# Two mixer blocks of a one-core network: two sparse-attention units' scores and maxima moved ahead of the state-space heads

## The chip, the cores and the metric

The kernel runs on one core of one Trainium2 chip. The metric is the device time of one execution in microseconds (us), as the median of three runs. Engines are called by their names: TensorE (PE in the profile), VectorE (DVE), ScalarE (ACT), GpSimd (POOL) and SyncE (SP, which issues the DMAs of weights).

## The reference, cut to what matters

The program is a two-layer block (state-space mixer, short convolution, sparse attention, gated feed-forward) followed by a second network. The change touches only the mixers of the two layers of the first block. There 256 tokens of 1024 features are projected by `w_in`, three mixers run on parts of the projection, and their outputs, side by side, go through `w_out`:

```python
for l in range(DEPTH):
    h = rmsnorm(x, attn_norm_w[l])
    proj = h @ w_in[l]
    ...
    y_ssd = ssd_mixer(z, xbc, dt_raw, ...)       # 8 heads of 64, 2 groups, state 128
    y_sc = sc_b * causal_dwconv(sc_c * sc_h, sc_conv_w[l])
    y_nsa = nsa_mixer(q, k_c, v_c, k_s, v_s, k_w, v_w, g_nsa, ...)   # 4 heads of 64
    x = x + jnp.concatenate([y_ssd, y_sc, y_nsa], axis=-1) @ w_out[l]
```

In the state-space mixer a head's output is `(decay * cb) @ xdt` with `decay = exp(segment sums)`; in the sparse attention each query block has a softmax over 15 compressed keys, one over the selected keys and one over the window (at 256 tokens both of these see the same causal keys), and the three outputs are summed by gates.

## The kernel before, in words

Weights are float32. Each weight panel of 128x2048 is loaded into one of four `raw` slots by SyncE (slot after slot, L469 waits until the slot of four transfers ago is free), copied by ScalarE into a high part (`high`, L1317), and VectorE subtracts to give the low part (`low`, L1991); there are two slots of high and low parts, so `high` of a panel waits until the panel two before it has been used by TensorE. A product is three matmuls (`mm3`, L509): high by high, high by low, low by high. TensorE is the engine on which nearly all time is spent.

Every engine has its own queue, written out by hand in the order in which it runs (`mixers(l)` exists once for TensorE, L812; ScalarE, L1640; VectorE, L2461). There is no planner: an instruction late in its queue cannot pass one before it. Semaphores tie the queues together.

On TensorE the projection by `w_in` is cut into steps (`in_steps(a, b)`, L828): a step is one `mm3` of 256 columns, 16 steps make a panel, panels are counted j = 0 to 11, so panel j holds the steps 16j to 16j+15. From panel 9 on all panels write bank 0: step 160 waits until ScalarE has evacuated panel 9, step 176 until it has evacuated panel 10 (L835). Between groups of steps stand the small matmuls of the mixers:

- `scores(u)`, L883: scores of sparse unit u (there are 4: two pairs of heads by two blocks of 128 queries; units 0 and 2 see 128 keys and are called narrow here, 1 and 3 see 256 and are called wide). It waits for the maxima of unit u-1, because all units use banks 2 and 3; the compressed scores stand in `compressed(u)`, L437.
- VectorE's `maxes(u)`, L2621, ScalarE's `exps(u)`, L1728, VectorE's `probs(u)`, L2636, TensorE's `flips(u)`, L952 (transposes), ScalarE's `copies(u)`, L1740, TensorE's `product(u)`, L970, ScalarE's `out(u)`, L1750: the chain of one unit.
- `spread(t)`, L929, ScalarE's `ssd_gap(t)` and `ssd_exp(t)`, L1712 and L1723, VectorE's `mats(t)`, L2663, TensorE's `head_pair(t)`, L941, VectorE's `out(t)`, L2669: the chain of one of the four pairs of state-space heads. Banks 2 to 5 alternate for `spread`.
- In layer 0 alone, `spread_condition(i)`, L874, and ScalarE's `condition(i)`, L1671, prepare the second network's condition vector; the group matmuls of g = 1 (L923) wait for the last of them, as they take bank 7.
- At the end `norm(4, ...)`, L1025, sums the squares of the state-space output, and `out_part(n, MIXED)`, L987, starts the output projection: its eight inputs k come in the order `MIXED` = 6, 4, 5, 0, 1, 2, 3, 7, where 6 and 7 are sparse attention, 4 and 5 the short convolution and 0 to 3 the state-space output. Step k waits for the low part of input k (`mixed_low`, L2675).

ScalarE evacuates a finished panel (`evacuate(j)`, L1647) and makes the high part of the panel two later (`ahead(j)`, L1664); the order of ScalarE's queue from the first pair of heads on is written out from L1766. VectorE's is from L2681. The lines in ScalarE's queue that the steps below lean on, and which stand after the part that the change edits, are:

```python
evacuate(10)
copies(1)
ahead(10)
exps(3)
out(1)
copies(2)
run(root_warm[:, :], eps[:, :], ACT.Sqrt)
evacuate(11)
out(2)
nsa_high(0)
root_y()
copies(3)
```

Of the kernel before, what the change touches and what calls it, by code (L numbers as in the profile page):

```python
# [12 lines left out]
P = 128  # L13
# [230 lines left out]
def two_blocks(nc, xT, ctxT, params_d, consts_d, weights, out_d):  # L244
    ctx = ExitStack()
    with ctx:
# [75 lines left out]
        cond_diag = sb("cond_diag", [P, 2, 512], at=A + 4096)  # L322
# [114 lines left out]
        def compressed(u):  # L437

            return bank[1][:, 0:2 * N_CMP] if u else bank[2][:, T:T + 2 * N_CMP]
# [62 lines left out]
        def _(pe):  # L502
# [309 lines left out]
            def mixers(l):  # L812
# [70 lines left out]
                def scores(u):  # L883
                    i, _, qs, W = nsa_unit(u)
                    if u == 0:
                        pe.wait_ge(S("kv_ready"), l + 1)
                    else:
                        pe.wait_ge(S("nsa_max"), n0 + u)
                    if u == 1:
                        pe.wait_ge(S("ssd_gap"), d + 3)  # L890
                    for r in range(2):
                        for h2, rows in enumerate(halves):
                            mm(bank[2 + h2][:, r * W:(r + 1) * W], krq[rows, 2 + i, qs], krq[rows, r ^ h2, 0:W], True, True)
                    mm(compressed(u), krq[:, 2 + i, qs], kc[:, :, :].rearrange("p h n -> p (h n)"), True,
                       True).then_inc(S("nsa_scored"), 1)
# [15 lines left out]
                in_steps(132, 144)  # L911
                spread_condition(3)
# [3 lines left out]
                for tb in range(2):  # L916
                    for t in range(4):
                        last = nc.tensor.transpose(bank[4 + tb][:, t * P:(t + 1) * P], xc[:, t, tb * P:(tb + 1) * P], ident)
                    last.then_inc(S("x_turned"), 1)
                pe.wait_ge(S("xbc_ready"), x + 8)  # L920
                pe.wait_ge(S("kv_ready"), l + 1)
# [7 lines left out]
                def spread(t):  # L929
                    if t == 0:  # L930
                        pe.wait_ge(S("nsa_max"), n0 + 1)
# [76 lines left out]
                scores(1)  # L1008
                in_steps(160, 162)
                head_pair(3)  # L1010
                flips(0)
                in_steps(162, 166)
                scores(2)
                product(0)
                in_steps(166, 176)
                flips(1)
                scores(3)
                in_steps(176, 182)
                product(1)
                flips(2)  # L1020
                in_steps(182, 188)
                product(2)
                in_steps(188, 192)
                pe.wait_ge(S("nsa_max"), n0 + 4)
                norm(4, T, 512, o=1)  # L1025
                flips(3)
                product(3)
                ws[0] = panel(L + "_out", 0)
                pe.wait_ge(S("in_evac"), e + IN_PANELS)
                out_part(0, MIXED)  # L1030
# [277 lines left out]
        def _(act):  # L1308
# [331 lines left out]
            def mixers(l):  # L1640
# [125 lines left out]
                exps(0)  # L1766
                ssd_gap(0)
                ssd_exp(0)
                ssd_gap(1)
                ssd_exp(1)  # L1770
                ahead(8)
                ssd_gap(2)
                ssd_exp(2)
                evacuate(9)
                ssd_gap(3)
                ssd_exp(3)
                ahead(9)
                copies(0)
                exps(1)
# [203 lines left out]
        def _(dve):  # L1983
# [15 lines left out]

            def entry_low(name, n, i):  # L2000
# [27 lines left out]
            def mod_part(name, n, s):  # L2028
# [6 lines left out]
                link(V.tensor_tensor_reduce(products[:, :], raw[slot][:, 0:DM], cond[:, s, :], 1.0,  # L2035
# [425 lines left out]
            def mixers(l):  # L2461
# [110 lines left out]
                def in_low(j):  # L2572
                    low(f"l{l}_in", IN_ORDER[j])
# [108 lines left out]
                in_low(9)  # L2682
                for tb in range(2):
# [7 lines left out]
                if l:  # L2691
                    mod_part("l1_in", IN_ORDER[7], 0)
                else:
                    probs(0)
                mats(0)
                if l:
                    mod_part("l1_in", IN_ORDER[7], 1)
                mats(1)
                in_low(10)
                out(0)  # L2700
                mats(2)
                out(1)
                if l:
                    probs(0)
                mats(3)
                out(2)
                maxes(1)
                out(3)
                maxes(2)
                in_low(11)  # L2710
                probs(1)
                probs(2)
                maxes(3)
                short_conv(0)
                short_conv(1)
                probs(3)
# [4 lines left out]
                rms(4, T)  # L2721
                y2 = take("ssd_high", 4)
# [3 lines left out]
                mixed_low(0)  # L2726
                mixed_low(1)
# [369 lines left out]
```

## Time and profile before

| what | value |
|---|---|
| median of three runs | 2322.64 us (2322.52 to 2324.76) |
| time of the profiled execution | 2321.22 us |
| its span in the trace | 2319.4 us |
| TensorE, VectorE, ScalarE busy | 2263.3, 1699.2, 948.2 us |
| mixers of layer 0 from its last projection panels to the output projection | about 76 to 129 us |
| the same in layer 1 | about 408 to 460 us |

Times in the rows are us from the start of the span. A row of the timeline gives the start, the length, the engine, the source line, the operation with what it writes and reads, how many instructions were merged, and in brackets how long the engine had been idle before it and whom it waited for. Matmuls overlap, and the end of one is modelled: the distance from one start to the next is the time that TensorE's queue really takes, and an idle time in brackets is some 0.15 us shorter than the delay of the start. Line L507 is the helper of all matmuls and L1312 that of all ScalarE operations, so rows are told apart by their tiles: `sb_decays` are the state-space heads, `sb_nP` and `sb_nPT` the sparse units, `sb_hx_hi` with `sb_w_hi` projection steps.

### The profile page before, as it was taken

The page shows a single profiled execution, that of the slowest core. Times are in us where ns is not written, and L with a number is a line of the kernel's source. Part 1 is how long each engine was busy: PE and PEld are TensorE (multiplying, and loading weights), DVE is VectorE, ACT ScalarE, POOL GpSimd, SP SyncE. Part 2 cuts the span into 40 slices and gives each one's busy share as a digit, 9 for nine tenths or more (in the row PEclk, how much of TensorE's full clock was granted, in tenths as well). Part 3 has the DMA queues.
Part 4 walks back from the last instruction along what each step waited for, and adds up shares of the span by engine and source line. Part 5 has one row for each costly group of instructions (what it writes and reads, how often), then busy time and mean ns, then how long its engine had stood idle before and what let it go on. Part 6 is the DMA issues. An engine that isn't in the chain of part 4 may idle for free.

```text
span 2319.4 us, 35091 instructions
## 1 busy us (share of the span) xinstructions
PE 2263.3 (98%) x14334; PEld 2007.8 (87%) x14334; DVE 1699.2 (73%) x2781; ACT 948.2 (41%) x1408; POOL 112.7 (5%) x77
## 2 busy tenths in 40 slices
PE   7999999899999999999999999999999999999998
PEld 7799999799998888888778888888888888979997
DVE  6889978889989848845455883884884663796775
ACT  4766635766652222235553221222321222475343
POOL 0010010010110000010001000001000001001001
PEclk9999999999999999999999999999999999999999
DMA  6445475355545545532111553453454452313443
GB/s 248 164 146 182 156 257 190 116 200 183 175 170 192 189 154 182 181 127 87 51 73 55 182 186 129 166 182 127 147 196 157 137 176 105 144 40 124 181 157 121
DMA packets 66560, 355.83 MB, mean 153 GB/s; under 512 B 7136, under 2 KB 10208, under 8 KB 42336
## 3 DMA queue, kind: packets, MB, share of 16 engines
q1 hardware_dynamic: 66400, 353.60, 43.7%
q8 instruction: 113, 1.85, 0.3%
q14 instruction: 47, 0.39, 0.0%
HBM read 352.52 MB, written 1.05 MB: 152 GB/s over the span
## 4 chain that ended last, share of the span: by engine, by line
PE 87%; DVE 9%; ACT 2%; issue 1%; DMA 0%; DVEq 0%; ACTq 0%
PE bank L507 87%; DVE sb_w_lo L1997 3%; ACT sb_w_hi L1312 1%; DVE sb_products L2019 1%; DVE sb_swS L2882 1%; DVE sb_swP L2896 0%; PE bank L1154 0%; DVE sb_rstd L2067 0%; ACT sb_mid L1312 0%; DVE sb_normed L2076 0%; DMA sb_res<-x 0%; DVE sb_mid L2554 0%; DVE sb_latP L2787 0%; DVE sb_normed L2113 0%; DVE sb_nP L2655 0%
## 5 line engine op out<-in xcount | busy, mean ns | idle before, releaser
L1997 DVE TENSOR_TENSOR sb_w_lo<-sb_raw,sb_w_hi 128x2048 fp32r<-128x2048 f32 (+2 forms) x282 | 568.8, 2017 | 137.4 <-ACT sb_w_hi L1312 134.2
L1312 ACT ACTIVATE sb_w_hi<-sb_raw 128x2048 fp32r<-128x2048 f32 (+3 forms) x296 | 491.7, 1663 | 385.8 <-PE bank L507 384.4
L507 PE MATMUL bank<-sb_f_pair,sb_w_hi 128*128 128x256 f32 (+1 forms) x2090 | 523.1, 339 | 5.2 <-DVE sb_w_lo L1997 4.2
L507 PE MATMUL bank<-sb_h_hi,sb_w_hi 128*128 128x512 f32 (+1 forms) x1400 | 510.7, 365 | 1.9 <-DVE sb_w_lo L1997 1.6
L507 PE MATMUL bank<-sb_h_lo,sb_w_hi 128*128 128x512 f32 (+1 forms) x1400 | 507.3, 362 | 0.0
L507 PE MATMUL bank<-sb_h_hi,sb_w_lo 128*128 128x512 f32 (+1 forms) x1400 | 507.2, 362 | 0.0
L507 PEld LDWEIGHTS bank<-sb_f_pair,sb_w_hi 128*128 128x128 f32 x2090 | 360.2, 190 | 51.0 <-DVE sb_w_lo L1997 7.2
L2019 DVE CUSTOM_DVE_ANT_0 sb_products<-sb_raw,sb_cond,sb_params 128x1024 f32<-128x1024 f32 x284 | 365.2, 1286 | 33.4 <-DVEq L2021 16.9
L507 PE MATMUL bank<-sb_f_pair,sb_w_lo 128*128 128x256 f32 (+1 forms) x1122 | 365.9, 326 | 0.0
L507 PEld LDWEIGHTS bank<-sb_h_hi,sb_w_hi 128*128 128x128 f32 x1400 | 264.2, 189 | 44.5 <-DVE sb_w_lo L1997 2.2
L507 PEld LDWEIGHTS bank<-sb_h_lo,sb_w_hi 128*128 128x128 f32 x1400 | 264.2, 189 | 41.5 <-issue 0.5
L507 PEld LDWEIGHTS bank<-sb_h_hi,sb_w_lo 128*128 128x128 f32 x1400 | 264.2, 189 | 40.7
L507 PE MATMUL bank<-sb_raw_hi,sb_w_lo 128*128 128x256 f32 (+1 forms) x910 | 257.1, 283 | 0.0
L507 PE MATMUL bank<-sb_raw_hi,sb_w_hi 128*128 128x256 f32 (+1 forms) x910 | 256.8, 282 | 0.0
L507 PE MATMUL bank<-sb_raw_lo,sb_w_hi 128*128 128x256 f32 (+1 forms) x910 | 256.6, 282 | 0.0
L1312 ACT ACTIVATE sb_sil<-bank 128x512 f32<-128x512 f32 x66 | 39.4, 597 | 530.5 <-PE bank L507 530.5
L507 PEld LDWEIGHTS bank<-sb_f_pair,sb_w_lo 128*128 128x128 f32 x1122 | 212.8, 190 | 17.9
L495 POOL TENSOR_TENSOR sb_sq_sum<-sb_sq,sb_sq_sum 128x256 f32<-128x256 f32 (+1 forms) x68 | 111.9, 1646 | 2191.5 <-ACT sb_sq L1312 2191.0
L2175 DVE SCALAR_TENSOR_TENSOR sb_res<-bank,sb_modT,sb_res 128x256 f32<-128x256 f32 x112 | 49.8, 480 | 167.7 <-PE bank L507 166.8
L507 PEld LDWEIGHTS bank<-sb_raw_hi,sb_w_hi 128*128 128x128 f32 x910 | 172.4, 189 | 0.2 <-issue 0.2
L507 PEld LDWEIGHTS bank<-sb_raw_lo,sb_w_hi 128*128 128x128 f32 x910 | 172.2, 189 | 0.1
L507 PEld LDWEIGHTS bank<-sb_raw_hi,sb_w_lo 128*128 128x128 f32 x910 | 171.7, 189 | 0.0
(310 smaller groups left out, 2909.2 us busy)
## 6 DMA issues: line engine op xcount, KB each, us to landing
sb_raw<-w_mod SPq DMA_DIRECT2D x144, 512.0 KB, 3.3
sb_raw<-w_l_up SPq DMA_DIRECT2D x44, 1024.0 KB, 4.8
sb_raw<-w_l_in SPq DMA_DIRECT2D x24, 1024.0 KB, 7.0
sb_raw<-w_l_down SPq DMA_DIRECT2D x32, 704.0 KB, 4.1
sb_raw<-w_m0a_up SPq DMA_DIRECT2D x22, 1024.0 KB, 4.7
sb_raw<-w_m0b_up SPq DMA_DIRECT2D x22, 1024.0 KB, 4.7
sb_raw<-w_m1a_up SPq DMA_DIRECT2D x22, 1024.0 KB, 4.8
sb_raw<-w_m1b_up SPq DMA_DIRECT2D x22, 1024.0 KB, 4.8
```

Of the source, the lines that this page charges most:

```text
L495: nc.gpsimd.tensor_tensor(sq_sum[:, a:b], sq[:, k % 2, a:b], sq_sum[:, a:b], ALU.add).then_inc(S("sq_added"), 1)
L507: return nc.tensor.matmul(out, lhsT, rhs, start=start, stop=stop, skip_group_check=True)
L1312: return nc.scalar.activation(out, in_, func, **kw)
L1997: V.tensor_tensor(split_part(*at, w_lo[s]), landed_part(*at, raw[raw_slot(*at)]), split_part(*at, w_hi[s]).bitcast(F32), ALU.subtract).the ...
L2019: link(V.tensor_tensor_reduce(products[:, :], raw[slot][:, 0:DM], cond[:, s, :], 1.0, par("mod_b", g, g + 1), ALU.mult, ALU.add, modT[:, g ...
L2175: last = V.scalar_tensor_tensor(res[:, k, at:at + T], src[:, at:at + T], mod(l, c, k, s), res[:, k, at:at + T], ALU.mult, ALU.add)
L2882: ins = V.tensor_tensor_reduce(swS[:, u % 2, h2, :], bank[2 * (u % 2) + h2][:, :], sq[:, b, :], 1.0, -3e38, ALU.add, ALU.max, s[:, h2:h2 + 1])
```

## The change

TensorE: unit 1's scores move from behind `head_pair(2)` to behind step 135, before the first pair of heads; the transposes of x move ahead of steps 140 to 143, the last condition spread behind them; unit 2's scores move ahead of steps 162 to 165; unit 1's flips and unit 3's scores come one step earlier (before step 175); unit 2's product comes three steps earlier (before step 185); the norm's sum and unit 3's flips come before steps 188 to 191. The first output panel is run over inputs 6, 4, 5 for both of its tiles, then over the rest.

ScalarE: `exps(0)` moves from the very front to behind the first two pairs of heads (layer 0), or behind the third pair and `evacuate(9)` (layer 1); `evacuate(9)` moves behind the fourth pair in layer 0; in layer 0 the high part of the panel of j = 10 is made by VectorE (`high`, new); `exps(1)` comes before `copies(0)`; the high part of j = 11 comes after these.

VectorE: `maxes(1)` moves to the front, `probs(0)` behind `mats(2)`, `probs(1)` before the low part of j = 11, `probs(3)` between the two short convolutions, the low parts of the short convolution before the scaling of the state-space output. Buffers move so that unit 1's scores can live that early.

```diff
-        cond_diag = sb("cond_diag", [P, 2, 512], at=A + 4096)
+        cond_diag = sb("cond_diag", [P, 2, 512], at=H + 16384)
+        products_in = sb("products_in", [P, DM], at=A + 8192)
...
-            return bank[1][:, 0:2 * N_CMP] if u else bank[2][:, T:T + 2 * N_CMP]
+            return (bank[2][:, T:T + 2 * N_CMP], bank[6][:, 384:384 + 2 * N_CMP], bank[1][:, 0:2 * N_CMP])[min(u, 2)]
...
-                    if u == 1:
+                    if u == 2:
                         pe.wait_ge(S("ssd_gap"), d + 3)
...
                 scores(0)
                 spread_condition(2)
-                in_steps(132, 144)
-                spread_condition(3)
+                in_steps(132, 136)
+                scores(1)
+                in_steps(136, 140)
 
                 pe.wait_ge(S("xbc_ready"), x + 4)
                 pe.wait_ge(S("acs_ready"), l + 1)
...
                     last.then_inc(S("x_turned"), 1)
+                in_steps(140, 144)
+                spread_condition(3)
                 pe.wait_ge(S("xbc_ready"), x + 8)
-                pe.wait_ge(S("kv_ready"), l + 1)
+                pe.wait_ge(S("nsa_max"), n0 + 2)
...
                     if t == 0:
-                        pe.wait_ge(S("nsa_max"), n0 + 1)
+                        pe.wait_ge(S("nsa_max"), n0 + 2)
...
                 head_pair(2)
-                scores(1)
                 in_steps(160, 162)
                 head_pair(3)
                 flips(0)
+                scores(2)
                 in_steps(162, 166)
-                scores(2)
                 product(0)
-                in_steps(166, 176)
+                in_steps(166, 175)
                 flips(1)
                 scores(3)
-                in_steps(176, 182)
+                in_steps(175, 181)
                 product(1)
                 flips(2)
-                in_steps(182, 188)
+                in_steps(181, 185)
                 product(2)
-                in_steps(188, 192)
+                in_steps(185, 188)
                 pe.wait_ge(S("nsa_max"), n0 + 4)
                 norm(4, T, 512, o=1)
                 flips(3)
+                in_steps(188, 192)
                 product(3)
                 ws[0] = panel(L + "_out", 0)
                 pe.wait_ge(S("in_evac"), e + IN_PANELS)
-                out_part(0, MIXED)
+                out_part(0, MIXED[:3])
+                out_part(0, MIXED[3:])
...
-                exps(0)
-                ssd_gap(0)
-                ssd_exp(0)
-                ssd_gap(1)
-                ssd_exp(1)
-                ahead(8)
+                for t in range(2):
+                    ssd_gap(t)
+                    ssd_exp(t)
+                if l:
+                    ahead(8)
+                else:
+                    exps(0)
                 ssd_gap(2)
                 ssd_exp(2)
-                evacuate(9)
+                if l:
+                    evacuate(9)
+                    exps(0)
                 ssd_gap(3)
                 ssd_exp(3)
+                if l == 0:
+                    evacuate(9)
+                exps(1)
+                copies(0)
+                if l == 0:
+                    act.wait_ge(S("high"), SPLIT_AT["l0_in", IN_ORDER[10]] + 1)
                 ahead(9)
-                copies(0)
-                exps(1)
                 out(0)
...
+            def high(name, n):
+
+                dve.wait_ge(S("panels_used"), SPLIT_AT[name, n] - 1)
+                for at in raws_of(name, n):
+                    dve.wait_ge(S(f"landed{raw_slot(*at)}"), landed_value(*at))
+                    last = V.tensor_copy(split_part(*at, w_hi[half_slot(name, n)]), landed_part(*at, raw[raw_slot(*at)]))
+                last.then_inc(S("high"), 1)
...
                 maxes(0)
                 in_low(9)
+                maxes(1)
...
                 if l:
                     mod_part("l1_in", IN_ORDER[7], 0)
+                    mats(0)
+                    mod_part("l1_in", IN_ORDER[7], 1)
+                    mats(1)
+                    out(0)
+                    in_low(10)
+                    mats(2)
+                    out(1)
                 else:
-                    probs(0)
-                mats(0)
-                if l:
-                    mod_part("l1_in", IN_ORDER[7], 1)
-                mats(1)
-                in_low(10)
-                out(0)
-                mats(2)
-                out(1)
-                if l:
-                    probs(0)
+                    high("l0_in", IN_ORDER[10])
+                    mats(0)
+                    in_low(10)
+                    mats(1)
+                    out(0)
+                    out(1)
+                    mats(2)
+                probs(0)
                 mats(3)
                 out(2)
-                maxes(1)
                 out(3)
                 maxes(2)
+                probs(1)
                 in_low(11)
-                probs(1)
                 probs(2)
                 maxes(3)
                 short_conv(0)
+                probs(3)
                 short_conv(1)
-                probs(3)
                 low(f"l{l}_out", 0)
                 mixed_low(2)
                 short_gate(0)
                 short_gate(1)
                 rms(4, T)
+                mixed_low(0)
+                mixed_low(1)
...
-                mixed_low(0)
-                mixed_low(1)
```

## Rows read from the trace of the kernel before

**Rows 1.** The page: busy shares, and shares of the chain that ended last.

```profile
PE 2263.3 (98%) x14334; PEld 2007.8 (87%) x14334; DVE 1699.2 (73%) x2781; ACT 948.2 (41%) x1408; POOL 112.7 (5%) x77
...
PE 87%; DVE 9%; ACT 2%; issue 1%; DMA 0%; DVEq 0%; ACTq 0%
```

**Rows 2.** Waits in 64 to 130 us, layer 0: total us, times, longest.

```profile
PE bank L507 <- DVE sb_decays L2667: 1.8, 2, 1.0
...
PE bank L964 <- DVE sb_nP L2655: 1.6, 1, 1.6
```

**Rows 3.** The same view for 395 to 461 us, layer 1.

```profile
PE bank L507 <- DVE sb_decays L2667: 1.9, 3, 0.7
```

**Rows 4.** Timeline of TensorE, layer 0.

```profile
83.84 1.47 PE L507 MATMUL bank<-sb_mid 128*128 128x256 f32 x8
...
116.04 0.43 PE L507 MATMUL bank<-sb_mid,sb_vc 15*64 15x128 f32 x4
...
118.02 0.36 PE L507 MATMUL bank<-sb_hx_hi,sb_w_hi 128*128 128x256 f32 x1
...
120.34 0.43 PE L507 MATMUL bank<-sb_mid,sb_vc 15*64 15x128 f32 x4
...
122.83 0.59 PE L507 MATMUL bank<-sb_sq_sum,sb_inv 128*128 128x256 f32 x2
...
125.89 0.43 PE L507 MATMUL bank<-sb_mid,sb_vc 15*64 15x128 f32 x4 [0.94 <-ACT sb_mid L1312]
```

**Rows 5.** Timeline of TensorE, layer 1: third and fourth pair of heads.

```profile
427.68 0.87 PE L507 MATMUL bank<-sb_decays,sb_mid 128*64 128x256 f32 x8 [0.72 <-DVE sb_decays L2667]
...
431.40 0.87 PE L507 MATMUL bank<-sb_decays,sb_mid 128*64 128x256 f32 x8 [0.65 <-DVE sb_decays L2667]
```

**Rows 6.** Timeline of ScalarE, layer 0.

```profile
83.17 1.11 ACT L1312 ACTIVATE sb_cond<-bank 128x128 f32<-128x128 f32 x4 [0.26 <-PE bank L507]
...
112.00 1.12 ACT L1312 ACTIVATE sb_nPT<-bank 128x512 f32<-128x512 f32 x2 [1.24 <-PE bank L966]
...
113.28 1.90 ACT L1312 ACTIVATE sb_w_hi<-sb_raw 128x2048 fp32r<-128x2048 f32 x1
...
115.82 0.51 ACT L1312 ACTIVATE sb_nP<-sb_nP,sb_stat 128x256 f32<-128x256 f32 x1 [0.64 <-DVE sb_stat L2634]
...
118.88 0.36 ACT L1312 ACTIVATE sb_mid<-bank 15x256 f32<-15x256 f32 x1
...
123.03 0.77 ACT L1312 ACTIVATE sb_mid<-bank 128x512 f32<-128x512 f32 x2 [2.28 <-PE bank L507]
...
125.48 0.36 ACT L1312 ACTIVATE sb_mid<-bank 15x256 f32<-15x256 f32 x1
```

**Rows 7.** Timeline of ScalarE, layer 1.

```profile
415.51 0.40 ACT L1312 ACTIVATE sb_nP<-sb_nP,sb_stat 128x128 f32<-128x128 f32 x1
...
417.46 1.32 ACT L1312 ACTIVATE sb_decays<-bank,sb_acs 128x256 f32<-128x256 f32 x4
...
427.00 0.60 ACT L1312 ACTIVATE sb_mid<-bank 128x512 f32<-128x512 f32 x1 [1.30 <-PE bank L507]
...
427.49 1.35 ACT L1312 ACTIVATE sb_decays<-bank,sb_acs 128x256 f32<-128x256 f32 x4
...
428.87 0.84 ACT L1312 ACTIVATE sb_decays<-sb_decays 128x768 f32<-128x768 f32 x1
```

**Rows 8.** Timeline of VectorE, layer 1: the fourth pair's product.

```profile
430.39 0.95 DVE L2667 TENSOR_TENSOR sb_decays<-sb_decays,sb_cbT 128x768 f32<-128x768 f32 x1
```

**Rows 9.** Groups by line and form on VectorE: busy us, mean ns.

```profile
L1997 DVE TENSOR_TENSOR sb_w_lo<-sb_raw,sb_w_hi 128x2048 fp32r<-128x2048 f32 x170 | 389.2, 2289 | 76.8 <-ACT sb_w_hi L1312 75.2 <-DVE sb_prod L2415 0.7 <-DVEq L2021 0.4
...
L2871 DVE COPY sb_sq<-sb_consts 128x512 f32<-128x512 f32 x1 | 0.4, 427 | 0.0
```

**Rows 10.** Timeline of TensorE after a pause between the layers.

```profile
349.93 0.55 PE L507 MATMUL bank<-sb_w_hi,sb_hx_hi 128*128 128x256 f32 x1 [4.09 <-DVE sb_hx_lo L2088]
...
350.28 0.41 PE L507 MATMUL bank<-sb_w_lo,sb_hx_hi 128*128 128x256 f32 x1
```

**Rows 11.** Windows: us, busy of PE, PEld, DVE, ACT, POOL, granted clock, DMA.

```profile
351.00:353.00 2.00, 2.00 (x11) 2.00 (x11) 2.00 (x6) 1.20 (x3) 0.00 (x0) 0.50 0.01 4
```

More of the change, by code:

```diff
@@ L2034, in mod_part @@
                     dve.wait_ge(S("raw_free"), RAW_AT["mod", g] + RAW)
-                link(V.tensor_tensor_reduce(products[:, :], raw[slot][:, 0:DM], cond[:, s, :], 1.0,
+                out = products_in if name.endswith("_in") else products
+                link(V.tensor_tensor_reduce(out[:, :], raw[slot][:, 0:DM], cond[:, s, :], 1.0,
                                             par("mod_b", g, g + 1), ALU.mult, ALU.add, modT[:, g, s:s + 1]))
```

## The prediction

> **What bounds the kernel now.** I read the page first: TensorE is busy for 98% of the span and carries 87% of the chain that ended last [rows 1]. So other engines matter only where they make TensorE wait, and the other views were read for that: the waits of TensorE in the two stretches of the mixers, then the timelines of the three engines around each wait. What the reader should see is how little there is to win. Before the last projection step of layer 0, TensorE waits 1.8 us for the heads' decays and 1.6 us for unit 1's probabilities [rows 2]; in layer 1, where the probabilities cost the same, 1.9 us and 1.6 us [rows 3]. The delay of a start is some 0.15 us longer than its modelled idle time, and there are three waits in layer 0 and four in layer 1, so the true delays are about 3.4 + 0.5 = 3.9 us and 3.5 + 0.6 = 4.1 us. Behind the last step (call its end S; 122.83 us in layer 0) come the norm's sum and unit 3's flips, a wait of 0.94 us, and unit 3's product at S + 3.06 [rows 4]. Between the mixers' outputs and the next block TensorE runs without a pause, so a shift of S passes on whole.
>
> **Measure and base.** The sum is made against the profiled execution, 2321.22 us; the median of three is 2322.64 us, 1.42 us more. I add the shift to the median. About 0.2%, 4.6 us, is what a measurement can tell from no change.
>
> **What goes.** With unit 1's scores and maxima done before the heads, and ScalarE starting with the heads instead of `exps(0)` (1.95 us, from 415.51 to 417.46 [rows 7]), the heads' first two pairs are ready when TensorE comes to them. Unit 1's exponentials now precede `copies(0)`, so its probabilities are ready by its flips. I count all the old delays as gone: -3.9 - 4.1 = -8.0 us. That is the most that can go. No matmul is removed or added; the four moved scores and sixteen transposes change place only.
>
> **What comes, at five places.**
>
> (a) *Condition (layer 0).* The transposes used to stand between the last condition spread and the group matmuls. Now `cb` of g = 1 comes 0.86 (the spread) + 0.70 (g = 0, half of the 1.40 us of the row at 83.84 [rows 4]) = 1.56 us after the spread begins, but waits for ScalarE's last `condition`, which began 1.06 us after the spread's begin and takes 1.11 us [rows 6]: 2.17 + 0.05 - 1.56 = 0.65 us. The 0.86 and 1.06 are from starts not shown; as bounds, 0 if hidden, 1.1 if all of `condition` shows.
>
> (b) *Fourth pair, layer 0.* ScalarE now evacuates panel 9 behind the fourth pair's exponentials, and VectorE makes `probs(0)` before `mats(3)`. Following the queues from the transposes with these durations, step 160 waits 0.5 us and `head_pair(3)` 0.55 us: 1.05 us, from 0 to 2.
>
> (c) *Fourth pair, layer 1.* This is the big one. ScalarE's queue is `evacuate(9)`, `exps(0)`, `ssd_gap(3)`, `ssd_exp(3)`. The evacuation waits for step 159. If TensorE ends it at X, the evacuation starts at X + 0.2 and frees ScalarE after 0.49 us (427.00 to 427.49), `exps(0)` takes 1.95, the gap 1.38 (427.49 to 428.87), the exponential 0.84 [rows 7]; VectorE's product 0.95 [rows 8], plus 0.1 of semaphores: X + 5.9. TensorE has only `head_pair(2)` (0.80) and steps 160 and 161 (0.8) to do: X + 1.65. So it pauses 4.25 us. Before, `scores(1)` stood here as cover and `exps(0)` did not stand in the chain: the fourth pair came 3.72 us behind the third with a wait of 0.65 [rows 5]. ScalarE meanwhile sits idle ahead of the evacuation, as before (1.30 us [rows 7]). Bounds: 3 to 5 us.
>
> (d) *Step 175 before step 176, both layers.* Steps 175 and 176 were parted by unit 1's flips and unit 3's scores, which hid the evacuation of panel 10, for all panels from 9 on share bank 0. Now 176 follows 175 directly: 0.2 + 0.6 (the evacuation's length at 427.00 [rows 7]) + 0.05 = 0.85 us each. From the end of 175, T, ScalarE then runs the evacuation to T + 0.7, `copies(1)` 1.28 (112.00 to 113.28), the high part 1.80, and `exps(3)`, `out(1)` and `copies(2)` together 3.42 (115.82 to 118.88 + 0.36 [rows 6]): T + 7.2. TensorE does 0.85 of waiting, five steps (1.9), `product(1)` and `flips(2)` (1.98, 116.04 to 118.02), four steps (1.55; six take 2.32, 118.02 to 120.34 [rows 4]): T + 6.25. `product(2)`, three steps earlier than before, waits 0.95 us. Together 1.8 us a layer, 3.6 in all; from 1.7 (the evacuation alone) to 5.
>
> (e) *The end, both layers.* ScalarE's `evacuate(11)` waits for step 191, and `copies(3)` stands behind it, so `copies(3)` is done only at S + 3.0, from the row at 123.03 to the end of the one at 125.48 [rows 6]. Before, TensorE filled 3.06 - 0.94 = 2.1 us of that with the norm and unit 3's flips. Now these stand ahead of the steps: S comes 2.1 us later and `product(3)` still comes at S + 3.06, after a wait of 3.05 us. The cost is 2.1 us a layer, 4.2 in all. The wait behind it is neutral: two tiles' worth of inputs 6, 4, 5 stand ready to be run, but the two early low parts delay VectorE's scaling by 0.8 us; I get the first output panel's end within 0.1 us of before, counted from S.
>
> **Costed at nothing.** VectorE's copy of one panel's high part in layer 0: between four times 0.43 us and the 2.29 us of the low part of the same size [rows 9]; it runs while VectorE would wait for the first pair's exponential, and only if it took over 2.3 us would `mats(0)` be late, by the excess. Where `probs(3)` stands ahead of a short convolution VectorE waits for `exps(3)`, with that convolution and the next low part queued behind; the low part is still done 0.1 us before S and is needed at S + 4.5. SyncE's transfers hang on VectorE's low parts: the last ones, for the output panels, keep their distance to S. The moved buffers change no duration.
>
> **Sum.** -8.0 + 0.65 + 1.05 + 4.25 + 0.2 (small waits at unit 1's scores and step 160 in layer 1) + 3.6 + 4.2 = +6.0 us; a walk along the queues without cancelling terms gives +6.4. I take +6.2: 2327.4 us for a run like the profiled one, 2328.8 us for the median.
>
> **Rivals.**
>
> *The clock falls in the pause.* After a pause of 4.09 us between the layers the matmuls started 0.2 us apart instead of 0.12 [rows 10], and the granted clock there was 0.50, 1.2 GHz [rows 11]. That pause had little work shortly before it; (c)'s 4.25 us stands behind dense work, so this is open. The price is from the same place: some 21 matmuls each 0.09 us longer, 2 us, or 3 if it begins late: +8.7, 2331.3 us. The Trainium skill's page "TensorE: Matmul & The Clock Gate", section "HAM oscillation — how this bites in real kernels", says that pauses in the matmuls bring the array back to half clock. By that rule the rival would be the forecast.
>
> *The pause of (c) is not there.* If the exponentials of unit 0 do not hold up the fourth pair (place: ScalarE between `evacuate(9)` and `ssd_gap(3)`), the sum is +2.0, 2324.6 us, no change by the bound. It decides where the pause is under 2.7 us. For it: everything before that place works as the change wants, and my X is computed; against it: five terms of it are read from rows and are in series by queue order.
>
> *The gain comes through.* (c), (d) and (b) vanish and only (e) stays: -8.0 + 4.2 = -3.8, 2318.8 us at best, which is still under the bound. For a gain over 4.6 us, (e) would have to be hidden too; ScalarE's order speaks against it.
>
> *The waits only change place.* TensorE's idle sum stays, since one engine's queue after another sets the pace in turn: +1, 2323.6 us.
>
> **Chances.** Forecast (+5 to +8) 0.50; clock falls 0.18; no pause 0.17; waits change place 0.12; gain 0.03. Slower by over 0.2%: the first two, 0.68. Within: 0.30. Faster: 0.02, out of the gain's 0.03, in case (e) is hidden as well. The range leaves out the gain and the upper end of the clock: 2323.0 to 2332.5 us.
>
> **What would show it.** In the changed trace: no wait for `sb_decays` ahead of the first two pairs; in layer 1 a wait of about 4 us ahead of the fourth; in both layers a wait of 0.8 us for the evacuation at step 176, of 1 us at the product of unit 2, and of 3 us at the last product, with `sb_mid` of ScalarE as releaser; no wait for `sb_nP`. The prediction is wrong if the fourth pair of layer 1 starts less than 3 us behind step 161, or if the last product's wait is near the old 0.94 us.

## The result, and the profile after

The changed kernel takes 2333.82 us (median of 5 runs, 2330.51 to 2336.01) against 2322.64 us before: +11.2 us, a ratio of 1.0043 (95% interval 1.0032 to 1.0054). Forecast were +6.2 us, 2328.8 us, with an upper end of 2332.5. The sign was right, the size was not. The profiled run took 2334.02 us, with a span of 2332.2.

First the page, as in [rows 1]; then the waits of TensorE in layer 1, 395 to 475 us (total us, times, longest), as in [rows 3]. In the changed kernel L508 is the helper of all matmuls and L1317 that of all ScalarE operations; these numbers shift by a few lines from kernel to kernel.

```profile
PE 2272.3 (97%) x14334; PEld 2014.5 (86%) x14334; DVE 1701.0 (73%) x2782; ACT 946.8 (41%) x1407; POOL 113.1 (5%) x77
...
PE 88%; DVE 8%; ACT 2%; issue 1%; DMA 0%; SPq 0%; DVEq 0%; ACTq 0%
```

```profile
PE bank L508 <- ACT sb_mid L1317: 4.1, 3, 2.7
PE bank L508 <- DVE sb_decays L2688: 4.0, 1, 4.0
PE bank L508 <- DVE sb_w_lo L2009: 1.3, 1, 1.3
PE bank L508 <- DVE sb_hx_lo L2699: 0.4, 1, 0.4
```

No wait for `sb_nP` is left, and the one for `sb_decays` is a single one. But TensorE's busy time grew by 9.0 us (2263.3 to 2272.3) with the same 14334 matmuls: they became longer. That is no wait, and no term of my sum could give it (a second profiled run of the same kernel has 2272.3 too).

The timeline of TensorE in layer 0 has the waits of (a), (b), (d) and (e), in the order in which they come:

```profile
87.16 0.92 PE L508 MATMUL bank<-sb_mid 128*128 128x256 f32 x4 [0.53 <-ACT sb_cond L1317]
...
100.04 0.36 PE L508 MATMUL bank<-sb_hx_hi,sb_w_hi 128*128 128x256 f32 x1 [0.54 <-ACT sb_mid L1317]
...
101.22 0.87 PE L508 MATMUL bank<-sb_decays,sb_mid 128*64 128x256 f32 x8 [0.23 <-DVE sb_decays L2688]
...
113.49 0.36 PE L508 MATMUL bank<-sb_hx_hi,sb_w_hi 128*128 128x256 f32 x1 [0.78 <-ACT sb_mid L1317]
...
119.72 0.43 PE L508 MATMUL bank<-sb_mid,sb_vc 15*64 15x128 f32 x4 [0.62 <-ACT sb_mid L1317]
...
128.11 0.69 PE L508 MATMUL bank<-sb_mid,sb_vc 15*64 15x128 f32 x4 [2.72 <-ACT sb_mid L1317]
```

Compare the last row with that of unit 3's product in [rows 4]: the wait is 2.72 instead of 0.94 us, and the same four matmuls take 0.69 instead of 0.43. In layer 1 the third and the fourth pair of heads, as in [rows 5], and the first step behind `product(0)`, which is step 166:

```profile
431.64 0.87 PE L508 MATMUL bank<-sb_decays,sb_mid 128*64 128x256 f32 x8
...
437.42 1.55 PE L508 MATMUL bank<-sb_decays,sb_mid 128*64 128x256 f32 x8 [3.98 <-DVE sb_decays L2688]
...
445.99 0.39 PE L508 MATMUL bank<-sb_hx_hi,sb_w_hi 128*128 128x256 f32 x1
```

ScalarE there, as in [rows 7]: evacuation, `exps(0)`, gap, exponential, one behind the other as forecast; and the product of VectorE, as in [rows 8].

```profile
431.75 0.60 ACT L1317 ACTIVATE sb_mid<-bank 128x512 f32<-128x512 f32 x1 [1.57 <-PE bank L508]
432.24 0.39 ACT L1317 ACTIVATE sb_nP<-sb_nP,sb_stat 128x128 f32<-128x128 f32 x1
...
434.18 1.33 ACT L1317 ACTIVATE sb_decays<-bank,sb_acs 128x256 f32<-128x256 f32 x4
435.53 0.84 ACT L1317 ACTIVATE sb_decays<-sb_decays 128x768 f32<-128x768 f32 x1
```

```profile
436.41 0.96 DVE L2688 TENSOR_TENSOR sb_decays<-sb_decays,sb_cbT 128x768 f32<-128x768 f32 x1
```

The fourth pair starts 5.78 us behind the third (437.42 - 431.64). With X the end of step 159 I had it at X + 5.9. But its eight matmuls take 1.55 instead of 0.87 us. The windows say why (us, busy of PE, PEld, DVE, ACT, POOL, granted clock, DMA), first around the last product of layer 0, then in the pause of layer 1, its last line behind the last product of that layer:

```profile
126.00:128.00 2.00, 0.00 (x0) 0.00 (x0) 1.47 (x4) 2.00 (x8) 0.00 (x0) 1.00 0.78 229
128.00:130.00 2.00, 1.89 (x16) 1.56 (x18) 1.29 (x1) 2.00 (x3) 0.00 (x0) 0.52 0.71 299
...
134.00:136.00 2.00, 2.00 (x15) 2.00 (x15) 2.00 (x2) 0.00 (x0) 0.00 (x0) 0.78 0.00 0
```

```profile
434.00:436.00 2.00, 0.00 (x0) 0.00 (x0) 1.55 (x12) 1.97 (x7) 0.00 (x0) 0.82 0.27 115
436.00:438.00 2.00, 0.58 (x4) 0.39 (x6) 1.96 (x6) 2.00 (x8) 0.00 (x0) 0.50 0.01 4
...
444.00:446.00 2.00, 2.00 (x17) 1.27 (x16) 1.93 (x9) 0.00 (x0) 0.00 (x0) 0.62 0.00 0
446.00:448.00 2.00, 2.00 (x18) 2.00 (x17) 1.90 (x1) 1.89 (x10) 0.00 (x0) 1.00 0.00 0
...
470.00:472.00 2.00, 1.62 (x8) 1.54 (x8) 2.00 (x6) 1.01 (x4) 0.00 (x0) 0.50 0.00 0
```

The granted clock goes to 0.50 (1.2 GHz) towards the end of the first two pauses and stays there for about 7 and 10 us (from the shares in the windows: 128 to 135, and 435.3 to 445.5); behind the last product of layer 1 it is there for some 3.4 us. So two theories stood. **Waits and clock:** the waits cost what I had summed, and the rest is TensorE at half clock behind three pauses (the last product of each layer, the fourth pair of layer 1). **Waits alone:** the clock is a side show, and the rest is another loss.

### The profile page after: what moved, and what is told of

Same layout as the page of the kernel before. It is cut to its first block, busy times and chain, and to the rows that moved or that the text cites. A ratio compares the mean times of both kernels' runs of the same rounds, so it can differ in the third digit from the quotient of the medians.

```text
span 2332.2 us, 35090 instructions
## 1 busy us (share of the span) xinstructions
PE 2272.3 (97%) x14334; PEld 2014.5 (86%) x14334; DVE 1701.0 (73%) x2782; ACT 946.8 (41%) x1407; POOL 113.1 (5%) x77
## 3 DMA queue, kind: packets, MB, share of 16 engines
HBM read 352.52 MB, written 1.05 MB: 152 GB/s over the span
## 4 chain that ended last, share of the span: by engine, by line
PE 88%; DVE 8%; ACT 2%; issue 1%; DMA 0%; SPq 0%; DVEq 0%; ACTq 0%
PE bank L508 87%; DVE sb_w_lo L2009 2%; ACT sb_w_hi L1317 1%; DVE sb_products L2039 1%; DVE sb_swS L2907 1%; DVE sb_swP L2921 0%; PE bank L1159 0%; DMA sb_raw<-w_l_in 0%; ACT sb_mid L1317 0%; DVE sb_rstd L2088 0%; ACT sb_nPT L1317 0%; ACT sb_nP L1317 0%; PE bank L970 0%; DVE sb_normed L2097 0%; DVE sb_mid L2575 0%
## 5 line engine op out<-in xcount | busy, mean ns | idle before, releaser
L1317 ACT ACTIVATE sb_w_hi<-sb_raw 128x2048 fp32r<-128x2048 f32 (+3 forms) x295 | 489.9, 1663 | 386.4 <-PE bank L508 384.8
L508 PE MATMUL bank<-sb_f_pair,sb_w_hi 128*128 128x256 f32 (+1 forms) x2090 | 524.0, 339 | 5.2 <-DVE sb_w_lo L2009 4.2
L508 PE MATMUL bank<-sb_h_hi,sb_w_hi 128*128 128x512 f32 (+1 forms) x1400 | 510.7, 365 | 1.9 <-DVE sb_w_lo L2009 1.6
L508 PE MATMUL bank<-sb_h_lo,sb_w_hi 128*128 128x512 f32 (+1 forms) x1400 | 507.3, 362 | 0.0
L508 PE MATMUL bank<-sb_h_hi,sb_w_lo 128*128 128x512 f32 (+1 forms) x1400 | 507.2, 362 | 0.0
L508 PEld LDWEIGHTS bank<-sb_f_pair,sb_w_hi 128*128 128x128 f32 x2090 | 360.3, 190 | 51.9 <-DVE sb_w_lo L2009 7.2
L508 PE MATMUL bank<-sb_f_pair,sb_w_lo 128*128 128x256 f32 (+1 forms) x1122 | 366.1, 326 | 0.0
L508 PEld LDWEIGHTS bank<-sb_h_hi,sb_w_hi 128*128 128x128 f32 x1400 | 264.1, 189 | 44.3 <-DVE sb_w_lo L2009 2.3
L508 PEld LDWEIGHTS bank<-sb_h_lo,sb_w_hi 128*128 128x128 f32 x1400 | 264.2, 189 | 41.5 <-issue 0.5
L508 PEld LDWEIGHTS bank<-sb_h_hi,sb_w_lo 128*128 128x128 f32 x1400 | 264.2, 189 | 40.8
L508 PE MATMUL bank<-sb_raw_hi,sb_w_lo 128*128 128x256 f32 (+1 forms) x910 | 257.1, 283 | 0.0
L508 PE MATMUL bank<-sb_raw_hi,sb_w_hi 128*128 128x256 f32 (+1 forms) x910 | 256.8, 282 | 0.0
L508 PE MATMUL bank<-sb_raw_lo,sb_w_hi 128*128 128x256 f32 (+1 forms) x910 | 256.5, 282 | 0.0
L1317 ACT ACTIVATE sb_sil<-bank 128x512 f32<-128x512 f32 x66 | 39.5, 599 | 530.5 <-PE bank L508 530.5
L508 PEld LDWEIGHTS bank<-sb_f_pair,sb_w_lo 128*128 128x128 f32 x1122 | 212.7, 190 | 17.9
L508 PEld LDWEIGHTS bank<-sb_raw_hi,sb_w_hi 128*128 128x128 f32 x910 | 172.4, 189 | 0.2 <-issue 0.2
L508 PEld LDWEIGHTS bank<-sb_raw_lo,sb_w_hi 128*128 128x128 f32 x910 | 172.2, 189 | 0.1
L508 PEld LDWEIGHTS bank<-sb_raw_hi,sb_w_lo 128*128 128x128 f32 x910 | 171.7, 189 | 0.0
```

The source lines that it names most:

```text
L508: return nc.tensor.matmul(out, lhsT, rhs, start=start, stop=stop, skip_group_check=True)
L1317: return nc.scalar.activation(out, in_, func, **kw)
```

## The experiments

Each was timed in 5 to 11 runs; "against before" is median against median of the kernel before, timed beside it; the intervals are of the ratio of runs and need not centre on the ratio of the medians. Filling means matmuls into a free bank whose result is not read; nothing is left out for them.

**The changed kernel again.**

> The changed kernel as it is, as the base of this call. Theory (waits and clock): the waits cost some +6 us, as forecast, and TensorE at half clock behind three pauses (the two last products and the fourth pair of layer 1) some +5: 2333 to 2335 us, +11 against the kernel before. Rival (waits alone; the rest came from something that changes from run to run): nearer to +6, 2329 us.

2332.59 us, +10.3 against before (ratio 1.0042, 1.0029 to 1.0054). This is the base of the next three.

**Filling in the pause of layer 1.**

```diff
                 in_steps(160, 162)
+                for _ in range(8 * l):
+                    mm(bank[1][:, 0:T], inv[1024][:, :], con("cos1"), True, True)
                 head_pair(3)
```

> Layer 1 only: eight matmuls whose result nobody reads (128 rows, 256 columns, float32, some 0.43 us each by the norm's sum, 3.4 us together) stand in the pause before the fourth pair. They do not move that pair, since it waits 3.98 us anyway. Waits and clock: the granted clock stays at 1.00 there, the 8.6 us from the pair to step 166 become 5.0, and the time falls by 3.0 to 3.6 us. Waits alone: no change, or +0.5 us if the filling overruns. Rival (a fall of the clock is only put off, and comes later in the layer): within 1 us of the changed kernel.

2328.53 us, 4.1 less than the base, where 3.0 to 3.6 were expected (7 runs of 2327.4 to 2330.5 against 5 of 2329.1 to 2333.1, so the size is rough). The timeline shows the same place with the same releaser, and a window there the clock:

```profile
436.12 0.87 PE L508 MATMUL bank<-sb_decays,sb_mid 128*64 128x256 f32 x8 [0.53 <-DVE sb_decays L2690]
```

```profile
436.00:438.00 2.00, 1.88 (x18) 1.34 (x20) 1.79 (x5) 1.92 (x9) 0.00 (x0) 1.00 0.01 4
```

The pair still comes 5.78 us behind the third (430.34), so the wait did not shrink; only the clock changed, and the time with it. From the pair to step 166 it takes 5.05 us (to 441.17) instead of 8.57. Waits alone falls.

**Filling in all three pauses** (as above, and six such matmuls ahead of `product(3)`, to bank 3).

> The same filling in layer 1's pause, and six such matmuls (2.6 us) in the wait before the last product in both layers. Waits and clock: no stretch at 0.50 from 83 to 475 us apart from the one between the layers, the waits for ScalarE and VectorE end at the same distances as before (last product at S + 2.9), and the time falls by 6.5 to 8 us against the changed kernel: 2326 to 2327.5, within 1.5 us of the +6 that the waits were forecast to cost in all. Waits alone: no change. If only the layer-1 pause matters: -3.3 us, as with the filling there alone.

2327.24 us, 5.35 less than the base, where 6.5 to 8 were expected, and +4.9 against before (1.0022, 1.0013 to 1.0031). All 11 runs lie below all 5 of the base. No stretch of the mixers shows a clock below 1.00. Two rows of TensorE's timeline serve as marks, the first wait for `sb_w_lo` in layer 1 (A) and the first in the network behind (B). Here they are in this kernel, and then in the changed one:

```profile
408.26 0.39 PE L508 MATMUL bank<-sb_hx_hi,sb_w_hi 128*128 128x256 f32 x1 [1.31 <-DVE sb_w_lo L2013]
...
651.49 0.50 PE L508 MATMUL bank<-sb_f_pair,sb_w_hi 128*128 128x256 f32 x2 [0.49 <-DVE sb_w_lo L2013]
```

```profile
410.38 0.38 PE L508 MATMUL bank<-sb_hx_hi,sb_w_hi 128*128 128x256 f32 x1 [1.33 <-DVE sb_w_lo L2009]
...
657.71 0.51 PE L508 MATMUL bank<-sb_f_pair,sb_w_hi 128*128 128x256 f32 x2 [0.50 <-DVE sb_w_lo L2009]
```

In the kernel before they stand at 406.49 and 645.78. So with the clock held up layer 0 costs +1.8 us (A) and layer 1 +3.9 us (B - A: 243.2 against 239.3). My terms were -3.9 + 0.65 + 1.05 + 1.8 + 2.1 = +1.7 and -4.1 + 4.25 + 0.2 + 1.8 + 2.1 = +4.25. In the changed kernel A is +3.9, of which 0.5 us stand already ahead of the first condition spread, and B - A is +8.0.

**The end's order put back**, with the pause of layer 1 left open, and then filled.

```diff
-                in_steps(185, 188)
+                in_steps(185, 192)
                 pe.wait_ge(S("nsa_max"), n0 + 4)
                 norm(4, T, 512, o=1)
                 flips(3)
-                in_steps(188, 192)
                 product(3)
```

> The norm's sum and unit 3's flips stand behind steps 188 to 191 again, as in the kernel before, in both layers; all else is as changed. Waits and clock: the last product comes at S + 3.0 from an S that is 2.1 us earlier, so -4.0 us for the waits; the pause is 0.9 us again and the clock does not fall, -2.8 us in layer 0 and -1.8 in layer 1: -8 to -9 us together. Waits alone: -4.0 to -4.2 us. Rival (ScalarE's queue as changed keeps its end where it is, whatever TensorE does): under -1 us.

2326.40 us, 6.2 less than the base, not 8 to 9. The wait ahead of the product is 0.94 again and the clock stays up there. At the fourth pair the wait is that of the changed kernel, yet the fall is shorter than there:

```profile
433.66 1.16 PE L508 MATMUL bank<-sb_decays,sb_mid 128*64 128x256 f32 x8 [3.98 <-DVE sb_decays L2687]
```

```profile
434.00:436.00 2.00, 2.00 (x14) 1.30 (x10) 1.33 (x3) 1.36 (x6) 0.00 (x0) 0.53 0.00 0
436.00:438.00 2.00, 2.00 (x14) 1.65 (x14) 0.17 (x1) 1.76 (x3) 0.00 (x0) 0.62 0.00 0
438.00:440.00 2.00, 2.00 (x23) 1.70 (x22) 1.83 (x21) 0.68 (x1) 0.00 (x0) 1.00 0.00 0
```

> The filling in layer 1's pause, and the old order at the end of both layers (norm and unit 3's flips behind step 191). Against the kernel with the filling in all three pauses this is the wait part of term (e) alone, since in neither should the clock fall: -4.0 to -4.2 us, 2323.1 us or +0.8 against the kernel before. Rival (with the clock held, the order at the end costs nothing, the norm and flips merely change places): equal to the filling in all three, 2327.2 us.

2324.69 us, +2.2 against before (1.0008, 0.9999 to 1.0016), so 2.7 less than the filling in all three (+4.9), where 4.0 to 4.2 were expected. In layer 0 the two stand 1.6 us apart at mark A (408.26 and 406.65), not 2.1: the wait part of (e) was set too high. In layer 1 this kernel's own profile has a fall at the end that the other has not (462:464 at 0.50), behind waits of 0.94 and 0.63 us only, which takes back part of the gain.

**Part (e) alone, in the kernel before** (norm and `flips(3)` ahead of steps 188 to 191).

> The kernel before, with one part of the change alone: the norm's sum and unit 3's flips moved ahead of steps 188 to 191, in both layers. Waits and clock: TensorE's wait ahead of the last product grows from 0.94 to 2.7 us in both layers (in the changed kernel this part's waits alone came to 1.7 us a layer: the kernels with the tail filled and with the tail put back stand 1.6 us apart at the end of layer 0), and the clock falls behind it, 1 to 3 us a layer: +5.5 to +9 us. Waits alone: +3.4 us. Rival (the part costs only because the rest of the change loads ScalarE's queue): under +1 us.

2330.47 us, +8.0 against before (1.0032, 1.0019 to 1.0044), within the 5.5 to 9 of waits and clock, and far over both others. At most 3.6 us of it are the two longer waits (2.72 instead of 0.94, twice), so some 4.4 are left for two falls, over three times what filling the same two pauses gave in the changed kernel (1.3). The five runs lie in two groups, 2327.9 to 2328.1 and 2330.5 to 2330.9; why the falls are dearer here is open. The wait and the slow matmuls are those of the changed kernel:

```profile
127.97 0.43 PE L507 MATMUL bank<-sb_mid,sb_vc 15*64 15x128 f32 x4 [2.72 <-ACT sb_mid L1312]
128.33 1.82 PE L507 MATMUL bank<-sb_nPT,sb_mid 128*64 128x128 f32 x16
```

**Unit 0's exponentials ahead of panel 9's evacuation** (the two steps of ScalarE swapped in layer 1).

> Layer 1: ScalarE makes unit 0's exponentials ahead of panel 9's evacuation instead of behind it; all else as changed. The exponentials then use the time in which ScalarE waited for step 159, and the fourth pair should come at X + 4.4 instead of X + 5.8, after a pause of 2.6 instead of 4.0 us. Waits and clock: -1.4 us by the wait; pauses of 2.7 us did bring the clock down in both layers' last product, so the fall stays, and the sum is -1.4 us; were the clock to stay up, -4.7 us. Rival (the place of the exponentials does not hold the fourth pair up): no change in that wait and 0 us.

2329.59 us, +7.1 against before (1.0026, 1.0016 to 1.0036), so about 3.1 less than the changed kernel (+10.3; the two intervals overlap). The third pair is at 429.67, the fourth:

```profile
433.77 0.87 PE L508 MATMUL bank<-sb_decays,sb_mid 128*64 128x256 f32 x8 [2.06 <-DVE sb_decays L2688]
```

X + 4.1 instead of 5.8: the place of the exponentials is what held the pair. The pause is halved, but the clock falls behind it all the same (0.75, 0.50, 0.50 and 0.55 in the windows from 434 to 442). The wait gave 1.7 us. Where the other 1.4 come from is not shown: from the pair to step 166 it takes 8.04 us here, and 7.97 in a second profiled run of the changed kernel, so the fall there did not get cheaper. What is shorter in the profiled run is the fall behind the last product of layer 0, which the swap does not touch (some 3 us at half clock instead of 7).

**Steps 175 and 176 parted again** (`in_steps(166, 176)` and `in_steps(176, 181)`).

> Steps 175 and 176 are parted by unit 1's flips and unit 3's scores again, in both layers. The term (d) of the forecast was 1.8 us a layer: no wait at step 176 and none at the product of unit 2, so -2.8 us (their modelled idle time, 0.78 + 0.62 in each layer) to -3.6 us. Rival (the product's wait does not hang on step 175's place, since it is ScalarE's queue that is full): only the evacuation's wait goes, -1.6 us. The clock: no pause of over 1 us is touched, no part in it.

2330.21 us, +7.7 against before (1.0026, 1.0018 to 1.0035), so about 2.5 less, where 2.8 to 3.6 were expected. The waits at step 176 (0.78) and ahead of unit 2's product (0.62) are gone in both layers. The runs fall into two groups, five at 2326.5 to 2327.0 and six at 2330.2 to 2333.4; the mean clock is 0.995 in the first and 0.992 to 0.994 in the second. The wait that went is clear, the size of the gain is blurred by the clock.

**One step of VectorE alone, in the kernel before** (`probs(1)` ahead of `in_low(11)`).

> The kernel before, with one step moved: VectorE scales unit 1's probabilities ahead of panel 11's low part (2.29 us) instead of behind it, in both layers. It asks whether the 1.6 us that TensorE waited for these probabilities needed the whole reordering. If they were late because of that low part alone: the waits for sb_nP go, -2.5 to -3.4 us against the kernel before. If ScalarE's exponentials of unit 1 were late themselves: -1 us or less. If the low part is then late in its place: a wait for sb_w_lo at step 176 and no gain, or +1 us.

2325.29 us, +2.8 against before (1.0008, 0.9999 to 1.0017, so no change is not excluded). It removes the 1.6 us waits and gains nothing:

```profile
112.75 0.36 PE L507 MATMUL bank<-sb_hx_hi,sb_w_hi 128*128 128x256 f32 x1 [0.35 <-ACT sb_mid L1312]
...
124.94 0.43 PE L507 MATMUL bank<-sb_mid,sb_vc 15*64 15x128 f32 x4 [0.94 <-ACT sb_mid L1312]
...
128.90 0.58 PE L507 MATMUL bank<-sb_hx_hi,sb_w_hi 128*128 128x256 f32 x1 [1.95 <-DVE sb_hx_lo L2678]
```

The last product comes 0.95 us earlier than in [rows 4], but the output projection starts where it did, at 128.9: VectorE's low parts end there, and TensorE waits 1.95 instead of 1.10 us. Behind that longer wait the clock falls in both layers (0.64 in 128:130, 0.50 in 460:462). None of my three branches had this. The change's early low parts might have met it; no run tried the two together in the kernel before.

**A version from these findings:** the end's order put back, the steps parted, and in layer 1 this order on ScalarE and TensorE (VectorE makes `mats(3)` and `out(2)` ahead of `probs(0)`).

```diff
-                if l:
-                    evacuate(9)
-                    exps(0)
                 ssd_gap(3)
                 ssd_exp(3)
-                if l == 0:
-                    evacuate(9)
+                evacuate(9)
+                if l:
+                    exps(0)
...
                 head_pair(3)
+                if l:
+                    in_steps(162, 166)
                 flips(0)
                 scores(2)
-                in_steps(162, 166)
+                in_steps(166 if l else 162, 168 if l else 166)
                 product(0)
```

> The changed kernel with its three costly places mended: the end's order put back, steps 175 and 176 parted, and in layer 1 ScalarE makes the fourth pair's exponentials, then panel 9's evacuation, then unit 0's exponentials, while TensorE takes steps 162 to 165 ahead of unit 0's flips and two more steps ahead of its product. Waits and clock: the fourth pair comes without a pause over 0.6 us (step 160 waits some 0.5 for the evacuation), flips of unit 0 wait up to 0.5; against the changed kernel with filled pause and old end (+2.2 us against before) this takes 1.7 us a layer off for the parted steps and some 3 us off layer 1: -3 to -4 us against the kernel before, 2318.5 to 2319.5. Rival (VectorE's chain of norm and low parts sets the start of the output projection, as when only the probabilities were moved): the gain turns into the wait ahead of the first output panel, and the time is within 1.5 us of before.

2319.32 us, -3.1 against before (0.9985, 0.9976 to 0.9994), where the changed kernel had +10.3. From 60 to 660 us only the windows around the pause between the layers show a clock below 1.00. The pause has shrunk to this:

```profile
427.49 0.36 PE L508 MATMUL bank<-sb_hx_hi,sb_w_hi 128*128 128x256 f32 x1 [0.48 <-ACT sb_mid L1318]
...
428.37 0.87 PE L508 MATMUL bank<-sb_decays,sb_mid 128*64 128x256 f32 x8
...
431.01 0.27 PE L968 MATMUL bank<-sb_consts,sb_nPC 128*15 128x128 f32 x1 [0.15 <-DVE sb_nP L2675]
```

> The same kernel, with two matmuls whose result nobody reads ahead of the last product and one behind it (0.4 us each), in both layers. In the fill-and-old-end kernel the granted clock still fell behind two short waits of 0.9 and 0.6 us at the end of layer 1, and in the kernel before with early probabilities behind 0.9 and 1.95 us. If that falls here as well, the filling takes 1 to 3 us off, and the runs lie closer together; if the clock stays up at the end by itself, the filling changes nothing or costs up to 0.4 us a layer.

2319.36 us, the same. The clock stays up at the ends by itself.

**The version with filling between the layers** (three such matmuls inside the norm between the layers, nine behind it).

> The mended kernel with filling in another place, where every kernel of this study, the one before included, goes to half clock: between layer 0 and layer 1. Three matmuls whose result nobody reads stand in the 1.65 us wait inside the norm and nine (3.8 us) in the 4.1 us wait behind it. Theory (a fall of the clock is a price that stands beside the wait, wherever it happens): the row's matmuls start 0.12 us apart from the first on instead of 0.21 for some 15 of them, and the time falls by 1 to 2 us against the mended kernel, to -4 to -5 us against before. Rival (the steps behind that wait are paced by VectorE's low parts, so a slow TensorE there is hidden): the clock stays up and the next wait for a low part takes the gain, 0 us.

2319.80 us, -2.5 against before (0.9989, 0.9980 to 0.9998): no gain. A window of each, first without, then with the filling:

```profile
348.00:350.00 2.00, 1.68 (x8) 1.71 (x9) 2.00 (x7) 1.13 (x3) 0.00 (x0) 0.50 0.00 0
```

```profile
348.00:350.00 2.00, 1.79 (x13) 1.40 (x13) 2.00 (x6) 1.37 (x5) 0.00 (x0) 1.00 0.09 37
```

And TensorE's next wait of each in the timeline, in the same order:

```profile
356.42 0.39 PE L508 MATMUL bank<-sb_hx_hi,sb_w_hi 128*128 128x256 f32 x1 [0.76 <-DVE sb_w_lo L2008]
```

```profile
356.93 0.39 PE L508 MATMUL bank<-sb_hx_hi,sb_w_hi 128*128 128x256 f32 x1 [2.12 <-DVE sb_w_lo L2012]
```

The clock is held, and the next wait for a low part takes all of it (the second run is 0.5 us behind the first already at its first condition spread, 65.98 against 65.51, so the step starts at the same distance in both). The rival was right here: this fall costs nothing, because VectorE, not TensorE, is what the next step waits for.

## Why the prediction was off

**What goes (-8.0): right.** The first three pairs of both layers come without a wait, and no wait for `sb_nP` is left.

**(a) and (b): right in kind.** 0.53 us for the condition (forecast 0.65); 0.54 + 0.23 for the fourth pair of layer 0 (forecast 1.05).

**(c), the wait: right.** 3.98 us of idle time (forecast 4.25), by the five terms in series. Taking one of them out of the series (`exps(0)` ahead of the evacuation) brought the pair 1.7 us closer.

**(d): nearly right.** 0.78 + 0.62 us a layer, with some 0.15 us each behind the modelled idle time 1.7 (forecast 1.8). The working took 1.80 us for the high part, where its row in [rows 6] has 1.90; unit 2's product waited less than the 0.95 us summed all the same.

**(e), the wait: too high.** 1.6 us in layer 0 (forecast 2.1; the product came at S + 2.88, not S + 3.06, and its idle time grew from 0.94 to 2.72, by 1.78); the wait behind the last product was not neutral, it went from 1.10 to 0.63 us with the old order at the end, by the early low parts.

**The waits together** came to +4.9 us by the medians of the kernel with all pauses filled, +5.7 by the marks, against +6.2. The two differ because the marks are of single runs: the profiled run of before was 1.1 us under the medians of its later measurements. Behind mark B a profiled run takes 1673.6 us (before, (e) alone, and the last version with either filling) or 1674.5 (the ten others). The last version is among the ten without filling and not with it, at equal medians (2319.32 and 2319.36), so these 0.9 us are not a cost of the change.

**What failed is the step that left the clock out of the sum.** I put the fall into a rival, with three errors. It had one place, (c); the waits of (e) and the clock were never brought together, though I had written 3.05 us for that wait. Its price, 2 to 3 us, came from the rows between the layers [rows 10, 11], where, as the last run shows, the fall is hidden by VectorE; at (c) the stretch from the pair to step 166 took 8.57 us (437.42 to 445.99) against 4.96 before, so 3.6 (3.0 in a second profiled run, 1.6 and 1.5 in those of the old end and of the parted steps), and the filling gave 4.1. And its chance was 0.18, because the pause "stands behind dense work"; the clock fell in all three kernels that had that pause of 3.98 us open. The Trainium skill's page "TensorE: Matmul & The Clock Gate", section "HAM oscillation — how this bites in real kernels", was on the right side: by its rule the rival would have been the forecast, and 0.50 in the window at 436 agrees. Even then the forecast would have been +8.7, 2331.3 us, 2.5 under the result. By the fillings the clock cost 5.35 us, 4.1 at (c) and 1.3 at the two ends, where the rival had 2.5 for (c) alone; the waits, 1.3 us lower than summed, hid part of that (4.9 + 5.35 is the +10.3 of the changed kernel's second measurement, against +11.2 in the first). The range left out the upper end of the clock by the same step.

**The other rivals** fell as they stood: the pause was there (3.98 us, over the 2.7 that decided), and the idle time did not merely change place.

## What to carry to other kernels

A wait of TensorE of a few us (2.06 to 3.98 here) can have two prices, its own length and the slower matmuls behind it; sum them apart, for every such wait, the ones that a reordering makes longer included. Filling with matmuls that nobody reads separates the two, since the waits stay and only the clock changes. Before a fall of the clock is counted, see what TensorE meets next: between the layers, where VectorE's low parts set the pace, it cost nothing. And take several runs: the same fall was of different length in different runs of one kernel.

## What the runs showed of the hardware beyond that

- Waits of 2.72 us were followed by a granted clock of 0.50 in both layers of the changed kernel and of the kernel with (e) alone, one of 2.06 us too (434 to 442 us), and one of 1.95 us with 0.94 before it, in both layers of the kernel with `probs(1)` moved.
- The same wait of 3.98 us at the same place was followed by half clock for some 10 and some 7 us in two profiled runs of the changed kernel, and for some 3.4 us in the kernels with the old end (about 434.1 to 437.5) and with the parted steps. So the length is not a matter of the kernel alone. The runs of these kernels are spread wider as well: 5.5 us in the changed kernel (0.992 to 0.995 mean clock, the slowest run at the lowest), 1.4 us with all pauses filled.
- Two waits in a row of 0.94 and 0.63 us were followed by 0.50 at the end of layer 1 in one kernel and by no fall in three others (the old end without filling, the last version with and without filling between the layers), each by one profiled run. What decides between them is open; no run was made for it.
